# A hybrid decoder layer on one core: the norm ahead of the FFN, block ends, and one gate unit moved

## The reference

```
ada = silu(c) @ w_ada + b_ada                 -> shift1, scale1, gate1, shift2, scale2, gate2
h   = rmsnorm(x) * (1 + scale1) + shift1
h @ w_in -> gq gk gv gr glr | aq ak av | ga gb
A: gated linear attention (4 heads, chunks of 64), rmsnorm, * silu(gr), @ w_branch_a
B: 3 groups of 8 heads, windows 128/512/2048, dilation 1/4/16, T5 bias,
   joined by their softmax denominators, @ w_branch_b
x  += gate1 * ((sigmoid(ga) * A + sigmoid(gb) * B) @ w_out)
h2  = rmsnorm(x) * (1 + scale2) + shift2
a, b = split(h2 @ w_up);  a = causal conv (width 3) of a
x  += gate2 * ((silu(a) * b) @ w_down)
y   = rmsnorm(x)
```

## Time and profile before

| | |
|---|---|
| median of 3 runs | 1250.01 us |
| profiled execution | 1249.03 us, its span 1247.3 us |
| TensorE busy | 1187.5 us, 95% |
| VectorE, ScalarE, GpSimd busy | 50%, 36%, 9% |
| mean granted TensorE clock | 0.981 of full |
| moved by the DMA engines | 229.39 MB, mean 184 GB/s |

### The profile page before, as it was taken

The page is one execution under the profiler, slowest core; times in us unless marked ns, Lnnn a source line. Parts: engine busy times, 40 slices in busy tenths (PEclk is TensorE's granted clock), DMA queues, the critical chain, the costliest instruction groups (busy, mean ns, idle before and its releaser), DMA issues. The chain is left out here.

```text
span 1247.3 us, 23079 instructions
## 1 busy us (share of the span) xinstructions
PE 1187.5 (95%) x9681; PEld 1117.0 (90%) x9681; DVE 617.7 (50%) x999; ACT 447.0 (36%) x652; POOL 107.6 (9%) x189
## 2 busy tenths in 40 slices
PE   5899999999989999999997899999999999999997
PEld 3878998888889998989886799989999999999997
DVE  4432134645415544266586365548655655633333
ACT  3264333454434342343343353224333333222222
POOL 0000010111011001100310011000110110010000
PEclk9899999999989999999998999988999999999999
DMA  9664459773364224423437478613888887256661
GB/s 304 207 211 140 136 171 347 248 216 120 104 190 137 94 94 136 136 87 110 158 125 222 175 232 288 203 35 102 282 291 259 264 285 236 80 191 222 224 227 69
DMA packets 166016, 229.39 MB, mean 184 GB/s; under 512 B 7644, under 2 KB 148342, under 8 KB 164636
## 3 DMA queue, kind: packets, MB, share of 16 engines
q1 hardware_dynamic: 148720, 123.72, 32.5%
q10 hardware_dynamic: 1684, 54.56, 12.0%
q0 software_dynamic: 15536, 50.01, 11.8%
HBM read 204.58 MB, written 81.87 MB: 230 GB/s over the span
## 5 line engine op out<-in xcount | busy, mean ns | idle before, releaser
L378 PE MATMUL ps<-actH,whi 128*128 128x260 f32 x2064 | 433.9, 292 | 12.1 <-PEq L1245 4.8
L378 PE MATMUL ps<-actH,wlo 128*128 128x260 f32 x2064 | 418.2, 284 | 0.0
L378 PE MATMUL ps<-actL,whi 128*128 128x260 f32 x2064 | 417.6, 284 | 0.0
L378 PEld LDWEIGHTS ps<-actH,whi 128*128 128x128 f32 x2064 | 320.4, 191 | 32.4 <-issue 26.6
L378 PEld LDWEIGHTS ps<-actL,whi 128*128 128x128 f32 x2064 | 321.0, 190 | 0.0
L378 PEld LDWEIGHTS ps<-actH,wlo 128*128 128x128 f32 x2064 | 320.8, 190 | 0.0
L362 DVE TENSOR_TENSOR wlo<-wraw,whi 128x2048 fp32r<-128x2048 f32 (+2 forms) x95 | 141.3, 1499 | 157.1 <-ACT whi L349 156.8
L349 ACT ACTIVATE whi<-wraw 128x2048 fp32r<-128x2048 f32 (+2 forms) x95 | 119.3, 1275 | 133.0 <-PE ps L378 90.0
L433 ACT ACTIVATE arena<-ps 128x520 f32<-128x520 f32 x74 | 44.5, 601 | 208.1 <-PE ps L378 193.1
L378 PE MATMUL ps<-gH,whi 128*128 128x260 f32 x352 | 71.1, 283 | 0.0
L378 PE MATMUL ps<-gH,wlo 128*128 128x260 f32 x352 | 70.8, 282 | 0.0
(11 more groups left out here) (339 smaller groups left out, 1365.8 us busy)
## 6 DMA issues: line engine op xcount, KB each, us to landing
wraw<-in_w_in SPq DMA_DIRECT2D x38, 1024.0 KB, 5.4
out_win_s<-in_cache_win ACTq DMA_DIRECT2D x16, 2046.0 KB
wraw<-in_w_up SPq DMA_DIRECT2D x44, 512.0 KB, 5.8
out_win_s<-in_cache_win ACTq DMA_DIRECT2D x8, 2044.0 KB
wraw<-in_w_ada SPq DMA_DIRECT2D x14, 1024.0 KB, 6.2
arena<-in_w_ada SPq DMA_DIRECT2D x10, 1024.0 KB, 12.7
raw_gates<-arena SPq DMA_DIRECT2D x24, 260.0 KB, 6.9
arena<-raw_gates POOLq DMA_DIRECT2D x24, 260.0 KB, 4.2
```

The source lines that it names most:

```text
L378: last = pe.matmul(ps[:, 2 * (n % 2) + a, 0:HT], wt, X[:, k0 + j, a * HT:a * HT + HT], start=begin and j == 0 and wt is hi and X is H, sto ...
```

## The change

- Every block is opened with `no_gpsimd_drain=True`: at its end the other engines drain, GpSimd doesn't, and the barrier is one of semaphores.
- One `ga` unit moves from attention stage 0 (now 8 units) to stage 2 (now 5 units: gb gb ga gb gb).
- adaLN units 22 and 23 join the stream behind the first and second unit of the output projection. Their own slots, loads and waits go.
- In the norm ahead of the FFN, VectorE adds a square ahead of the next tile's residual, not behind it, and TensorE repeats a matmul on the first up weights (`keep_busy`): 7 times after the first ten sums, 10 after the second ten, 16 at the start of the FFN block. Their product goes to a bank that the first up unit overwrites.
- Up to down: the last transpose waits for one copy fewer, and the wait for g is split between the halves of down.
- Tail: the sums over partitions are written in bank 3 with the helper, the order of the last turns changes with it, and ScalarE, not SyncE, issues the store of y_sample.

```diff
-    add("aq1 aq1 ga ak1 ga ak1 av1 ga av1", "att0")
+    add("aq1 aq1 ga ak1 ga ak1 av1 av1", "att0")
-    add("gb gb gb gb", "att2")
-    late = list(range(16, N_TAIL))
+    add("gb gb ga gb gb", "att2")
+    late = list(range(16, N_ADA))
...
-        with nc.Block() as block:
+        with nc.Block(no_gpsimd_drain=True) as block:
...
+        def keep_busy(pe, n):
+            x = U[G["up"][0]]
+            t, w0 = x["tile0"], whi[:, x["i"] % 2, :]
+            pe.wait_ge(hi_ready, x["i"] + 1)
+            pe.wait_ge(tile_read[owner[t - 2]], freed[t - 2])
+            for _ in range(n):
+                pe.matmul(ps[:, 2 * (t % 2), 0:HT], w0[:, 0:P], w0[:, 0:HT], start=True, stop=True)
...
-                issue_all(sp, G["bb"][0] + 3, G["wo"][2] + 1)
-                sp.wait_ge(s("mixed"), KD)
-                for a in range(N_TAIL, N_ADA):
-                    (load adaLN unit a into tail_slot)
-                issue_all(sp, G["wo"][2] + 1, G["up"][0] + 2)
+                issue_all(sp, G["bb"][0] + 3, G["up"][0] + 2)
...
+                        square_dve(dve, 1, 2 * j + m - 1, n2)
                         dve.wait_ge(pass_done, passes[n])
                         residual_dve(dve, n, 2 * j + m, 2 * KD)
-                        square_dve(dve, 1, 2 * j + m - 1, n2)
                     late_ada_dve(dve, u)
-                ada_dve(dve, N_TAIL, ada4)
...
-                ada_dve(dve, N_TAIL + 1, ada4)
-                ada_turn_dve(dve, N_TAIL)
...
-                ada_pe(pe, N_TAIL)
                 pe.wait_ge(s("sq_added"), KD - 2)
-                sums_pe(pe, 5, n2["t"], True)
+                sums_pe(pe, 5, 0, n2["t"], True)
+                keep_busy(pe, 7)
                 pe.wait_ge(s("sq_ready"), KD)
-                sums_pe(pe, 5, n2["sq"][:, (KD - 1) % 2, :], False).then_inc(s("sq_summed"), 1)
-                ada_pe(pe, N_TAIL + 1)
-                ada_turn_pe(pe, N_TAIL, ada4)
+                sums_pe(pe, 5, 0, n2["sq"][:, (KD - 1) % 2, :], False).then_inc(s("sq_summed"), 1)
+                keep_busy(pe, 10)
                 spread_root_pe(pe, 1, tok2)
...
-                ada_turn_pe(pe, N_TAIL + 1, ada4)
+                keep_busy(pe, 16)
                 first_unit()
...
-                pe.wait_ge(s("tail_tok"), KF - 1)
+                pe.wait_ge(s("tail_tok"), KF - 2)
-                pe.wait_ge(s("g_lo"), KF)
...
                         pe.wait_ge(lo_ready, vd0 + 2 * m + half + 1 + 4 * i)
+                        if m == 0 and first:
+                            pe.wait_ge(s("g_lo"), KF // 2 * (half + 1))
...
-                sp.wait_ge(s("y_tok"), 5)
-                sp.wait_ge(s("y_tok_dve"), 5)
-                sp.dma_start(o["y_sample"], ysst).then_inc(s("y_out"), 16)
+                act.wait_ge(s("y_tok"), 5)
+                act.wait_ge(s("y_tok_dve"), 5)
+                act.dma_start(o["y_sample"], ysst).then_inc(s("y_out"), 16)
```

More of the change, by code:

```diff
@@ L35 @@
 QC = 32
-N_HEAD, N_TAIL, N_ADA = 8, 22, 24
+N_HEAD, N_ADA = 8, 24
 ADA_ORDER = [0, 4, 1, 5, 2, 6, 3, 7] + list(range(N_HEAD, N_ADA))
@@ L555, in ada_turn_dve, with sums_pe @@
                               ALU.add).then_inc(ada_read, 1)
-        def sums_pe(pe, bank, part, first):
+        def sums_pe(pe, bank, col, part, first):
             for n in range(5):
                 m = P if n < 4 else NS
-                last = pe.matmul(ps[0:m, bank, n:n + 1], part[:, P * n:P * n + m], ones[:, 0:1], start=first and n == 0,
+                last = pe.matmul(ps[0:m, bank, col + n:col + n + 1], part[:, P * n:P * n + m], ones[:, 0:1], start=first and n == 0,
                                  stop=not first and n == 4, skip_group_check=True)
@@ L2111, in sigmoid_act @@
             act.activation(sg4[:, r % 2, :], raw4[:, r % 4, :], ACT.Sigmoid).then_inc(s("sg_ready"), 1)
-        tail_slot = [at(o, UW) for o in (8320, 8320 + UW)]
         LATE = G["bb"] + G["ba"] + G["wo"]
+        def keep_busy(pe, n):
[5 more added lines that the diff above has]
+                pe.matmul(ps[:, 2 * (t % 2), 0:HT], w0[:, 0:P], w0[:, 0:HT], start=True, stop=True)
         def late_ada_pe(pe, u):
             j = LATE.index(u)
-            if 16 + j < N_TAIL:
+            if 16 + j < N_ADA:
                 ada_pe(pe, 16 + j)
-            if 1 <= j <= N_TAIL - 16:
+            if 1 <= j <= N_ADA - 16:
                 ada_turn_pe(pe, 15 + j, ada4)
@@ L2124, in late_ada_dve @@
             j = LATE.index(u)
-            if 16 + j < N_TAIL:
+            if 16 + j < N_ADA:
                 ada_dve(dve, 16 + j, ada4)
-            if 1 <= j <= N_TAIL - 16:
+            if 1 <= j <= N_ADA - 16:
                 ada_turn_dve(dve, 15 + j)
-        with nc.Block() as block:
+        with nc.Block(no_gpsimd_drain=True) as block:
             @block.sync
             def _(sp):
-                issue_all(sp, G["bb"][0] + 3, G["wo"][2] + 1)
-                sp.wait_ge(s("mixed"), KD)
-                for a in range(N_TAIL, N_ADA):
-                    src = w["w_ada"][:, 2 * P * a:2 * P * a + 2 * P].rearrange("(k p) n -> p k n", p=P)
-                    sp.dma_start(tail_slot[a - N_TAIL].rearrange("p (k n) -> p k n", k=KD), src).then_inc(s("ada_tail_in"), 16)
-                issue_all(sp, G["wo"][2] + 1, G["up"][0] + 2)
+                issue_all(sp, G["bb"][0] + 3, G["up"][0] + 2)
             @block.gpsimd
@@ L2430, in _ @@
                 modulate_ffn_dve(dve, xT, n2)
-                ada_turn_dve(dve, N_TAIL + 1)
                 def gain(k):
@@ L2469, in _ @@
                 dve.wait_ge(s("sq_summed"), 2)
-                mean_dve(dve, ps[:, 1, YS:YS + 5], tok)
+                mean_dve(dve, ps[:, 3, YS:YS + 5], tok)
                 root_dve(dve, 2, tok)
@@ L2556, in _ @@
                     turn(n, range(KD - 1))
-                pe.wait_ge(s("x_new"), 2 * KD)
                 pe.wait_ge(s("sq_added"), 2 * (KD - 2))
+                sums_pe(pe, 3, YS, n3["t"], True)
                 pe.wait_ge(s("sq_ready"), 2 * KD)
-                last_sq = n3["sq"][:, (KD - 1) % 2, :]
-                for n in range(5):
-                    m = P if n < 4 else NS
-                    for x, part in enumerate((n3["t"], last_sq)):
-                        last = pe.matmul(ps[0:m, 1, YS + n:YS + n + 1], part[:, P * n:P * n + m], ones[:, 0:1],
-                                         start=x == 0, stop=x == 1)
-                last.then_inc(s("sq_summed"), 1)
+                sums_pe(pe, 3, YS, n3["sq"][:, (KD - 1) % 2, :], False).then_inc(s("sq_summed"), 1)
                 pe.wait_ge(s("gained"), KD)
                 for n in range(3):
+                    if n == 2:
+                        pe.wait_ge(s("ms_ready"), 3)
                     turn(n, [KD - 1]).then_inc(s("y_T"), 1)
-                turn(4, range(4))
-                pe.wait_ge(s("ms_ready"), 3)
-                turn(4, range(4, KD)).then_inc(s("y_T"), 1)
+                turn(4, range(KD)).then_inc(s("y_T"), 1)
                 for half in range(2):
```

3 lines of the change are left out of this document (removed).

## The result

The changed kernel takes 1240.63 us (median of 4 runs, 1239.84 to 1242.22), against 1250.10 before (4 runs beside it; the three on record ahead of the prediction had 1250.01): ratio 0.9921, interval [0.9907, 0.9935]. Faster, but by about half of what was predicted: 1232.3 us, range to 1238.6. The profiled execution took 1241.3 us, its span 1239.6, mean granted clock 0.986 (0.981 before).

A forecast was written before the change was run, and what follows sets the result against it. TensorE, busy 95%: only its waits and its time at the lower clock can shrink. 5.9 + 7.5 + 1.35 + 2.85 + 0.1 = 17.7 us off 1249.03 gives 1231.3, median 1.0 above: 1232.3 us, range 1228.8 to 1238.6.

The forecast's parts named there:

- Block ends: End of block one: without GpSimd's drain the wait shrinks by 3.6 us and the clock returns 2.3, sum 5.9.
- The gate unit: Unit moved from first to third attention stage: stall gives 5.5 us and its clock 2.0, sum 7.5.
- The stall gives 5.5: Third attention stage: TensorE's 6.2 us wait behind the stored gate tiles goes, less 0.7 left.
- It also took the clock down: Third attention stage: the 4 us after the stall stand near clock 0.5, so 2.0 us come back.
- Norm gap: Norm ahead of the FFN: output projection 3.1 us longer, modulation 6.4 us after its last matmul, net gain 1.35.
- the root at T + 4.6: Norm gap: root ready at T + 4.57, T being the end of the last dense output-projection matmul.
- spread at full clock 1.25: Norm gap: TensorE's spread of the root takes 1.25 us, ending at T + 5.9.
- rival B: Norm gap: clock falls in spite of the repeats, sums and spread cost 0.5 + 1.3 more: 1234.1 us; chance 0.12.
- Up to down: Between up and down projection: down's first half needs only g 0 to 10 and starts earlier, gain 2.85 us.
- Tail: End of the kernel: sample store leaves SyncE's queue, gain 0.1 us, bounds -0.3 to +0.2.
- A: Third attention stage: the gate store still waits for the value loads, the 7.5 shrink to 0: 1239.8 us; chance 0.13.
- C: End of block one: the barrier without drain still holds TensorE, 5.9 us lost: 1238.2 us; chance 0.06.

The follow-up runs named there:

- e2: Kernel before with only the block ends changed (no_gpsimd_drain=True at every block): 1247.72 us, ratio 0.997.
- e4: Kernel before with only the norm-gap changes (adaLN units 22 and 23 in the output projection, sums in order, repeats): 1252.76 us, ratio 1.0006.
- e10: Changed kernel with the 32 helper steps of attention stage 0 spread over 31 of its 32 places: 1244.71 us, ratio 0.9945.
- e13: Changed kernel with SyncE storing the gate tiles before the weight load in attention stage 2's last unit: 1240.82 us, ratio 0.9918.
- e1: The changed kernel run once more, whole and unaltered: 1239.79 us, ratio 0.9899 to before.
- e8: Changed kernel with the store of y_sample issued by SyncE again: 1241.76 us, ratio 0.993.
- e7: Changed kernel with a second ga unit moved from attention stage 0 to stage 2: 1249.42 us, ratio 0.9991.
- e12: Changed kernel with the last two helper steps of attention stage 0 together in its last place but one: 1239.42 us, ratio 0.9903.
- e9: Changed kernel without repeats and with the last adaLN unit back in the norm gap, behind the second sums: 1240.54 us, ratio 0.9918.
- e14: Changed kernel with no repeats, last adaLN unit in the gap, stage 0's last steps together, stores before load, sample store on SyncE: 1237.32 us, ratio 0.9877.

## Why the prediction was wrong

The direction held, and most of the mechanisms. The forecast was 8.3 us too low: 5.9 by the sum and 2.4 by the base, where a start 4.1 us longer is partly made up by a median 0.7 us under the profiled run instead of 1.0 over it.

- **Block ends (5.9).** Right by the profiles: 6.6 alone, and 6.2 in the whole if stage 0 gained there the 2.4 of e2 (head block 3.8). By e2's median it is 4.1. ScalarE's drain is what is late next. (5.33 less 2.9 is 2.4, not the 2.3 taken.)
- **The gate unit (7.5).** This is the step that failed: the clock that was to come back, and a stall put at nothing. It brought 3.8 in the whole (14.0 - 2.4 in stage 0, less 7.8), 4.3 alone. "The stall gives 5.5" held, shown by the wait of 0.9 against the predicted 0.8 (which the sum took as 0.7). "It also took the clock down ... 2.0 come back" did not: the fall at 671 us is gone, and another of 3.4 us comes at 689, worth 2.9 by the two profiles without it. And the new stall in the first attention stage, which the prediction bounded at 0 to 1 and the sum took at nothing, was the place of another 1.1 us (the end wait, 2.26 instead of 1.16), not in the steps but in the last place, since 32 steps in 32 places put VectorE's last step directly ahead of the barrier; moving that step took them back. 2.9 + 1.1 is 4.0, against 3.7 missing. Where the second fall starts can be said: in 10 of the 12 profiles with a moved unit, while the 24 short matmuls run or up to 0.5 us behind them; in 4 profiles of stage 2 as before, once (e4). In e10 and e13 the same matmuls stand there and the clock stays up. Why it falls in most and not in all is not settled, nor whether the moved unit makes it more frequent.
- **Norm gap (1.35).** The mix's 3.1 and the root at T + 4.6 came to the tenth. The spread did not: "spread at full clock 1.25" was 2.2, started late behind the repeats. That is rival B, which had a chance of 0.12, with one thing that it missed: repeats at half clock stand ahead of the spread. Eight profiles have the changed gap with all its repeats: in five (the changed kernel, e1, e4, e8, e10) the clock fell there, in three (e7, e12, e13) it stayed. These three have modulation at T + 6.75, near the 6.4 of the forecast, and a mix 0.9 to 1.2 us longer. So the term is about 0 in either case: mix and gap took 137.5 to 137.9 us in these, and 137.5 before.
- **Up to down (2.85).** Right: 2.87.
- **Tail (0.1).** 0.6 longer instead, outside my bounds of -0.3 to +0.2; half of it varies between profiles of the same code. It is not traced to an edit.
- **The base.** The sum was made against a profile with a start of 52.6 us and three runs at 1250.0. In 61 later runs of before, beside the experiments, the medians are 1250.8 to 1251.8, and the start is 53.7 to 56.9 us in all other profiles. The changed kernel's own start was 4.1 us longer. Late first transfers make a part of that: TensorE's second matmul comes at 9.82 instead of 8.80 us, and the one behind the third such wait at 14.38 instead of 12.86. The other 2.6 us are not explained.

```profile
9.82 0.38 PE L799 MATMUL ps<-cst,arena 74*128 74x74 f32 x1 [4.64 <-DMA cst<-in_fold]
```

- **The range.** It allowed for one failure at a time: A 7.5, C 5.9, B 1.8. The time came from three partial ones (gate unit, norm gap, tail), and a base that I had taken as exact.
- **By the medians** the four parts tried alone make 4.1 + 5.8 - 1.0 + 3.6 = 12.5 us, the whole 12.0 (e1). They add up, but they divide the gain between block ends and gate unit otherwise than the profiles do, by 1.5 to 2.5 us. That the gate term is the one that failed most rests on the profiles' stages.

## What to carry to other kernels

Here a stall's own length was a good forecast, and the clock that "comes back" with it was not: 2.0 us were counted, and a new fall at another place took 2.9. Let such a term go down to nothing in the range, and look where the next short or idle work stands. When work is moved out of a stage whose steps are dealt over places, look at the last place: what stands there is added to the barrier. Work that only keeps an engine busy is dear where it stands ahead of an instruction on the path: where the clock fell, the ten repeats held the spread up by 0.6 us, and the kernel without them was as fast. And one profile is a weak base for a forecast of under 1%: code that no edit touched differed by up to 4 us.

## What the runs showed of the hardware

- The lower clock level cost 1.7 to 6.8 us at a time, and the same code met it at different places or not at all (the end of stage 2 loses 0, 1.7 or 3.4 us, the changed norm gap 0 or 1.7, 5.1 without its repeats, and the gap of e9 and e14 1.7 and 6.8).
- It can fall while TensorE does not idle: at 689.3 us, in a run of 24 matmuls of 8 and 4 columns (686.99 to 690.4).
- Dense matmuls between one-column matmuls shortened the low stretch, but did not reliably keep the granted clock: the same code gave 0.76 from 830 to 837 us in one profile and 1.00 in another.
- GpSimd's drain at a block's end, 7.6 us, is not needed for the barrier here: without it the wait of 4.8 us was 1.2, ended by ScalarE's drain of 0.63.
- The start of this kernel, the same code in 16 profiles, took 52.6 to 56.9 us.
